# Roots of two norms moved to queries and scores, one half's query moved ahead, first picks listed in two parts

## What is computed

```
h = rmsnorm(x, norm_xa_g)            # x * rsqrt(mean(x*x) + eps) * g
x = x + softmax((h @ w_q) k^T * 128**-0.5) v @ w_o      # 4 heads of 128
h = rmsnorm(x, norm_ffn_g)
q = h @ peer_w_q                     # 8 heads, two halves of 128
s1, s2 = top16 of q . subkeys        # 128 keys for each half
top16 of the 256 sums s1 + s2  ->  experts e, g = softmax(top scores)
a = gelu(h . w_down[e]);  x = x + sum(g * a * w_up[e])
out = rmsnorm(x, final_g)
```

## Time and profile before

| | us |
|---|---|
| median of 3 runs (lowest to highest) | 1367.7 (1366.07 to 1367.84) |
| the profiled execution | 1363.8 |
| its span, first to last instruction | 1362.0 |
| TensorE busy | 1211.0 |
| VectorE busy | 931.7 |
| ScalarE busy | 521.3 |
| GpSimd busy | 292.9 |

### The profile page before, as it was taken

How to read it: one execution, slowest core, us unless ns; L and a number is a source line. 1 busy time by engine, 2 the same in 40 slices (tenths; PEclk the granted TensorE clock), 3 DMA queues, 4 the chain that set the end, 5 groups by cost and what they waited for, 6 DMA issues and landing times.

```text
span 1362.0 us, 17457 instructions
## 1 busy us (share of the span) xinstructions
PE 1211.0 (89%) x6452; PEld 885.4 (65%) x6452; DVE 931.7 (68%) x1815; ACT 521.3 (38%) x959; POOL 292.9 (22%) x261
## 2 busy tenths in 40 slices
PE   6999999999999999999898999898777777878775
PEld 7999998899988899998674555444232222323322
DVE  6765748876664675567687777767777776776655
ACT  4843236545543446645643322323222222222212
POOL 0000000000000000000024445455444444444420
PEclk9999999999999999999999999999999999999999
DMA  7554235544565645348649999999999999999994
GB/s 274 183 172 141 94 110 214 194 152 180 178 228 198 211 165 180 133 179 293 248 192 419 414 420 419 419 420 420 418 421 420 420 419 419 421 420 419 420 421 185
DMA packets 55787, 396.75 MB, mean 291 GB/s; under 512 B 6304, under 2 KB 6304, under 8 KB 8352
## 3 DMA queue, kind: packets, MB, share of 16 engines
q0 software_dynamic: 36864, 268.45, 47.6%
q1 hardware_dynamic: 17136, 119.42, 24.7%
q10 hardware_dynamic: 1712, 7.87, 1.6%
HBM read 394.67 MB, written 1.05 MB: 291 GB/s over the span
## 4 chain that ended last, share of the span: by engine, by line
PE 57%; DMA 28%; DVE 9%; ACT 4%; issue 2%; POOL 0%; DVEq 0%; SPq 0%; POOLq 0%; ACTq 0%
DMA R<-experts,IDX 28%; PE ps L534 25%; PE ps L1063 12%; PE ps L617 10%; PE ps L584 3%; DVE w_lo L1597 2%; PE ps L546 2%; DVE JUNK L2266 1%; PE ps L726 1%; PE ps L714 1%; ACT DIAG L1476 1%; ACT w_hi L1113 1%; PE ps L652 0%; DMA raw<-weights 0%; DVE eq L2243 0%
## 5 line engine op out<-in xcount | busy, mean ns | idle before, releaser
L1063 PE MATMUL ps<-R,DIAG 128*128 128x512 f32 x1020 | 479.4, 616 | 118.6 <-ACT DIAG L1476 118.4
L1063 PEld LDWEIGHTS ps<-R,DIAG 128*128 128x128 f32 x1020 | 189.0, 194 | 387.3 <-issue 195.8
L2420 POOL DMA_INDIRECT R<-experts,IDX x256 | 291.5, 1139 | 548.6 <-PE ps L1063 303.8
L2266 DVE CUSTOM_DVE_ANT_0 JUNK<-R,XN 128x1024 f32<-128x1024 f32 x256 | 313.6, 1225 | 138.7 <-DMA R<-experts,IDX 135.9
L1597 DVE TENSOR_TENSOR w_lo<-raw,w_hi 128x1024 fp32r<-128x1024 f32 x206 | 243.2, 1224 | 98.9 <-ACT w_hi L1113 95.6
L1113 ACT ACTIVATE w_hi<-raw 128x1024 fp32r<-128x1024 f32 x206 | 206.2, 1050 | 89.7 <-DMA raw<-weights 87.2
L534 PE MATMUL ps<-opC_lo,w_hi 128*128 128x256 f32 x544 | 155.3, 286 | 3.7 <-DVE opC_lo L1567 2.4
L534 PE MATMUL ps<-opC_hi,w_hi 128*128 128x256 f32 x544 | 154.7, 284 | 0.0
L534 PE MATMUL ps<-opC_hi,w_lo 128*128 128x256 f32 x544 | 154.6, 284 | 0.0
L1476 ACT ACTIVATE DIAG<-con,coef 128x128 f32<-128x128 f32 x255 | 88.6, 394 | 122.6 <-DVE coef L2276 122.3
L1468 ACT ACTIVATE act_d<-dots 128x2 f32<-128x2 f32 (+1 forms) x130 | 26.3, 203 | 273.6 <-DVE dots L2266 273.5
(11 more groups left out here) (352 smaller groups left out, 1643.4 us busy)
## 6 DMA issues: line engine op xcount, KB each, us to landing
raw<-weights SPq DMA_DIRECT2D x104, 1024.0 KB, 4.8
PQW<-weights SPq DMA_DIRECT2D x6, 1024.0 KB, 8.0
R<-experts,IDX POOLq DMA_INDIRECT x256, 31.4
LNR<-rows ACTq DMA_DIRECT2D x3, 1024.0 KB, 5.1
XF<-xT SPq DMA_DIRECT2D x2, 512.0 KB, 6.2
raw<-weights SPq DMA_DIRECT2D x2, 512.0 KB, 6.9
MEM<-mem ACTq DMA_DIRECT2D x1, 1024.0 KB, 7.7
XR<-x ACTq DMA_DIRECT2D x1, 1024.0 KB, 4.8
```

The costliest lines, as they stand in the source:

```text
L1063: mm = pe.matmul(psum[:, 4 + 2 * m + n, :], DIAG[:, k, :], rows_[:, D + n * 512:D + (n + 1) * 512], start=(it % 8 == 0 and k == 0), stop=True,
L2266: dve.tensor_tensor_reduce(out=JUNK[:, :], in0=rows_[:, 0:D], in1=XN[:, it // 8, :], scale=1.0, scalar=0.0, op0=ALU.mult, op1=ALU.add, acc ...
L2420: pool.indirect_dma_start(out=R[u][:, :], out_offset=None, in_=experts, in_offset=bass.IndirectOffsetOnAxis(ap=IDX[:, it, k:k + 1], axis=0 ...
```

## The change

The rows XN hold XR x gain only. The factor 1/root goes into the copies that follow: cross queries (QN), pick scores (SC) and the gelu's argument; rst holds it until then. scale_side becomes inverse_side, XN is not read and written again. turn_side transposes one column half at a time, as soon as its gain is there. side_half is one half block of side, so that TensorE's order can weave half 0's cross query between half blocks of the projection. Unit 11 goes to pick 0, unit 18 to pick 1, unit 8 to pick 2 once the cross values of half 1 are done. Step 0 is decoded in two parts of eight picks into eq0, with index writing IDX, and GpSimd waits for each part. In the tail the two gain multiplies write XN and the first stands ahead of the root.

```diff
         XO_END = half_end(PQ0 - 1)
-        OPENED = {0: (8, None), 1: (11, None), 2: (18, None)}
+        VALUES_END = "values"
+        OPENED = {0: (11, None), 1: (18, None), 2: (8, VALUES_END)}
         for n, u in enumerate((1, 2, 5, 6, 12)):
...
         R = {u: unit(f"R{u}", u, [P, 2 * D]) for u in sorted(_uses)}
+        eq0 = unit("eq0", 17, [P, 2, 16, 16], off=4096)
         DIAG = unit("DIAG", 19, [P, TOPK, P])
...
                 if name == "h4Ta":
-                    wait_wide(pe, "xo", 2)
+                    wait_wide(pe, "xo", 1 + j)
                 elif a >= 2 and not (name in TURNED and j >= 2):
...
             both_sides("wo2", opC, "m2")
-            side("wo2", opC, 1, 0)
-            side("wo2", opC, 1, 1, lambda: turn_side("h3T", 0, 0, 1))
-            cross_query(0, [(0, 0), (0, 1), (1, 0), (1, 1)])
-            turn_side("h3T", 2, 1, 2)
+            side_half("wo2", opC, 1, 0, 0, 0)
+            side_half("wo2", opC, 1, 0, 0, 1)
+            turn_side("h3Ta", 0, 0, 0, 1)
+            side_half("wo2", opC, 1, 0, 1, 0)
+            side_half("wo2", opC, 1, 0, 1, 1)
+            cross_query(0, [(0, 0), (0, 1)])
+            turn_side("h3Ta", 1, 0, 1, 2)
+            side_half("wo2", opC, 1, 1, 0, 0)
+            cross_query(0, [(1, 0), (1, 1)])
+            side_half("wo2", opC, 1, 1, 0, 1)
             query_turn(0)
+            side_half("wo2", opC, 1, 1, 1, 0)
             cross_scores(0, 0)
             cross_scores(0, 1)
-            cross_query(1, [(0, 0), (0, 1)])
+            side_half("wo2", opC, 1, 1, 1, 1)
+            turn_side("h3Tb", 0, 1, 0, 3)
             cross_turn(0, 0)
             cross_turn(0, 1)
-            cross_query(1, [(1, 0)])
+            cross_query(1, [(0, 0)])
             cross_values(0)
-            cross_query(1, [(1, 1)])
+            turn_side("h3Tc", 0, 1, 1, 4)
+            cross_query(1, [(0, 1), (1, 0), (1, 1)])
             has_lo(pe, "ax", 0)
...
             side("xo", AXo, 1, 0)
+            turn_side("h4Ta", 0, 0, 0, 5)
             cross_scores(1, 0)
             cross_scores(1, 1)
-            turn_side("h4Ta", 0, 0, 3)
+            turn_side("h4Ta", 1, 0, 1, 6)
             query(0, 0)
...
             head_scores(2, 0)
-            turn_side("h4Tb", 0, 1, 4)
+            turn_side("h4Tb", 0, 1, 0, 7)
+            turn_side("h4Tb", 1, 1, 1, 8)
             query(3, 0)
...
                 act.activation(rst[:, m:m + 1], rst[:, m:m + 1], ACT.Sqrt).then_inc(xn_sd, 1)
-                act.wait_ge(xn_r, turn)
-                act.activation(XN[:, m, 512:D], XN[:, m, 512:D], ACT.Copy, scale=rst[:, m:m + 1]
-                               ).then_inc(xn_act, 1)
             def cross_rows(m):
...
                     act.wait_ge(half_done, 2)
-                drain(act.activation(QN[:, m, :], bank(RING["xq"] + m), ACT.Copy), "xq", m)
+                act.wait_ge(xn_r, 1 + m)
+                drain(act.activation(QN[:, m, :], bank(RING["xq"] + m), ACT.Copy, scale=rst[:, m:m + 1]),
+                      "xq", m)
             def cross_across(m):
...
             square_side("wo2", 1, 0, 0)
+            ahead(xq)
+            hi_side(0, 0)
             square_side("wo2", 2, 1, 0)
-            ahead(xq)
+            upper_half(xq + 1, 0)
             square_side("wo2", 3, 0, 1)
+            upper_half(xq + 1, 1)
+            hi_side(0, 1)
             root_side(1, 0)
-            upper_half(xq + 1, 0)
-            hi_side(0, 0)
-            hi_side(0, 1)
-            upper_half(xq + 1, 1)
-            upper_half(xo, 0)
-            square_side("wo2", 4, 1, 1)
-            root_side(2, 1)
-            act.dma_start(LNR[:, 0, :], rows[7:8, :].rearrange("a n -> (a n)").partition_broadcast(P)
-                          ).then_inc(rows2_in, 16)
             cross_rows(0)
-            hi_side(1, 0)
-            hi_side(1, 1)
             cross_across(0)
...
             cross_exps(0, 1)
+            hi_side(1, 0)
+            cross_turned(0, 0)
+            upper_half(xo, 0)
+            act.wait_ge(xn_gain, 4)
+            act.dma_start(LNR[:, 0, :], rows[7:8, :].rearrange("a n -> (a n)").partition_broadcast(P)
+                          ).then_inc(rows2_in, 16)
+            square_side("wo2", 4, 1, 1)
+            warm(ACT.Sqrt)
+            hi_side(1, 1)
+            root_side(2, 1)
+            values_hi(0)
             upper_half(xo, 1)
-            cross_turned(0, 0)
             upper_half(xo + 1, 0)
             upper_half(xo + 1, 1)
-            values_hi(0)
             cross_rows(1)
             cross_across(1)
-            warm(ACT.Sqrt)
             square_side("xo", 1, 0, 0)
+            rows_across("h4Ta", 0)
             square_side("xo", 2, 0, 1)
             root_side(3, 0)
-            rows_across("h4Ta", 0)
             warm(ACT.Exp)
...
                 name = scores_of(j, m)
+                act.wait_ge(xn_r, 3 + m)
                 drain_aux(act.activation(SC[:, m, 2 * j:2 * j + 2, :], v3(batch(act, *name)[:, 0:T], 2),
-                                         ACT.Copy), *name)
+                                         ACT.Copy, scale=rst[:, m:m + 1]), *name)
             def gate_exp(it):
...
                 act.wait_ge(dot_done, it * TOPK + k1)
-                act.activation(act_d[:, par, k0:k1], dots[:, par, k0:k1], ACT.Gelu_apprx_tanh
-                               ).then_inc(gelu_done, 1)
+                act.activation(act_d[:, par, k0:k1], dots[:, par, k0:k1], ACT.Gelu_apprx_tanh,
+                               scale=rst[:, it // 8:it // 8 + 1]).then_inc(gelu_done, 1)
                 if it == 15 and k0 == TOPK - 1:
...
                 cs = slice(512 * g, 512 * g + 512)
-                st.do(dve.tensor_tensor(XN[:, m, cs], XR[:, m, cs], LNR[:, row, cs], ALU.mult))
+                dve.tensor_tensor(XN[:, m, cs], XR[:, m, cs], LNR[:, row, cs], ALU.mult).then_inc(xn_gain, 1)
             def mean_side(turn, m):
...
                                   ).then_inc(xn_ms, 1)
-            def scale_side(turn, m):
+            def inverse_side(turn, m):
                 dve.wait_ge(xn_sd, turn)
-                st.sync()
                 dve.reciprocal(rst[:, m:m + 1], rst[:, m:m + 1]).then_inc(xn_r, 1)
-                dve.wait_ge(xn_r, turn)
-                dve.tensor_scalar(XN[:, m, 0:512], XN[:, m, 0:512], rst[:, m:m + 1], None, ALU.mult
-                                  ).then_inc(xn_dve, 1)
             def cross_max(m, n):
...
                 drain_aux(dve.tensor_copy(H4[:, 4:8, m * P:(m + 1) * P], v3(batch(dve, name, 1), 4)), name, 1)
-            ahead_low(BLOCK["wo2"] + 3)
+            xq, xo = BLOCK["xq"], BLOCK["xo"]
+            low(BLOCK["wo2"] + 3, 0)
             dve.wait_ge(rows2_in, 16)
-            for m in range(MT):
-                residual_side("wo2", 1 + m, m, 0)
-            for m in range(MT):
-                gain_side(0, m, 0)
-            ahead_low(BLOCK["xq"])
+            residual_side("wo2", 1, 0, 0)
+            gain_side(0, 0, 0)
+            low(BLOCK["wo2"] + 3, 1)
+            low(xq, 0)
+            lo_side(0, 0)
+            low(xq, 1)
+            residual_side("wo2", 2, 1, 0)
             residual_side("wo2", 3, 0, 1)
+            gain_side(0, 0, 1)
+            low(xq + 1, 0)
+            lo_side(0, 1)
+            low(xq + 1, 1)
             mean_side(1, 0)
-            gain_side(0, 0, 1)
-            scale_side(1, 0)
-            lo_side(0, 0)
-            lo_side(0, 1)
-            ahead_low(BLOCK["xq"] + 1)
-            residual_side("wo2", 4, 1, 1)
-            mean_side(2, 1)
-            gain_side(0, 1, 1)
-            scale_side(2, 1)
-            low(BLOCK["xo"], 0)
-            lo_side(1, 0)
-            lo_side(1, 1)
+            gain_side(0, 1, 0)
+            inverse_side(1, 0)
             cross_max(0, 0)
...
             cross_weights(0, 1)
+            lo_side(1, 0)
             cross_turned(0, 1)
-            low(BLOCK["xo"], 1)
+            residual_side("wo2", 4, 1, 1)
+            gain_side(0, 1, 1)
+            low(xo, 0)
+            lo_side(1, 1)
+            mean_side(2, 1)
             values_lo(0)
-            low(BLOCK["xo"] + 1, 0)
-            low(BLOCK["xo"] + 1, 1)
+            inverse_side(2, 1)
+            low(xo, 1)
+            low(xo + 1, 0)
+            low(xo + 1, 1)
             residual_side("xo", 1, 0, 0)
...
             residual_side("xo", 2, 0, 1)
+            gain_side(1, 0, 1)
+            rows_across("h4Ta", 0)
             mean_side(3, 0)
-            gain_side(1, 0, 1)
-            scale_side(3, 0)
-            rows_across("h4Ta", 0)
+            inverse_side(3, 0)
             cross_max(1, 0)
...
                 st.then(dve.max(cv[:, 0:8], cflat))
-                st.then(dve.match_replace(sW[:, :], cv[:, 0:8], cflat, LOWEST))
-            def top_d(it):
+                if more:
+                    st.then(dve.match_replace(sW[:, :], cv[:, 0:8], cflat, LOWEST))
+            def top_d(it, more=True):
```

(59 more changed lines are left out.)

79 lines of the change are left out of this document (40 added, 39 removed).

## The result

The changed kernel takes 1360.63 us (median of 5 runs, 1359.59 to 1361.05); the kernel before, in its runs beside it, 1367.7 (1364.7 to 1369.0). The ratio is 0.9949, 95% interval 0.9933 to 0.9966: 7.0 us less, where 3.6 were forecast. The profiled execution of the changed kernel took 1360.63 us, its span 1358.9. Against the *profiled* execution of before (1363.8 us) that is 3.2 us.

What follows compares the result with a forecast made beforehand. The gather stream of 256 picks was taken to bound the kernel, early picks held by sums: 3.0 us from the earlier start and sums plus 0.6 from the tail gave 3.6, so 1367.7 became 1364.1 us, range 1360.0 to 1369.2.

Steps and rivals of the forecast that it cites:

- TensorE's wait for the third query's copy: Ahead of the sums TensorE waits 1.7 us, until 702.2 us, for the copy of half 0's third query.
- pairs of 128 elements: Decode of eight picks: two operations on 128 elements take about 0.5 us, so one decode takes 2.35 us.
- The walk: New engine order followed step by step from the old trace, good to 1.2 us: 3.6 us gained, 1364.1 us; chance 0.50.
- The release: Sums free the slots of picks 8 to about 30, so of the first list's 6.4 us lead 3.0 reach the end.
- 6.1 us as the least landing: A gather with nothing queued ahead takes at least 6.1 us from issue to landing; pick 9 lands at 723.2 us.
- the 3.4 us of the rival: Landing behind an empty queue takes 3.4 us at least; pick 9 lands at 720.5 us, kernel 1361.1 us; chance 0.15.
- The order edit: Half 0 first in TensorE's order: scores 4.5 us earlier, but the output projection of half 0 only 0.5 us earlier.
- The fall of the clock: Behind TensorE's 1.61 us gap before the first query, clock 0.50 loses 1.7 us, which the roots edit removes.
- Against which time: 3.6 us off the profiled 1363.8 gives 1360.2; the runs' median, 3.9 higher at 1367.7, gives the predicted 1364.1 us.
- The clock didn't fall ahead of the sums: Rival: clock falls behind TensorE's 1.7 us wait, sums start 1.8 us earlier instead of 3.2, 1365.5 us; chance 0.20.
- in the gaps of the new order: Rival: clock falls in TensorE's five gaps of 646 to 668 us, 1.7 us each, up to 1370.9 us; chance 0.07.
- the decode wasn't at its upper bound: Rival: each decode of eight picks takes 1 us longer (bound 3.4 us), gain 1.6 us, 1366.1 us; chance 0.08.

Runs made afterwards that it cites:

- earlyonly: The kernel before with the early list of 8 picks and its units alone: 1364.70 us against 1362.82, ratio 1.0007 (0.9998 to 1.0016).
- onelist: The changed kernel with the first 16 picks decoded in one piece again: 1358.96 us, ratio to the kernel before 0.9977 (0.9968 to 0.9987).
- before_again: The kernel before, unchanged, on a second occasion: 1362.65 us (1361.86 to 1365.35, 11 runs).
- after_again: The changed kernel, unchanged, on a second occasion: 1360.62 us (1359.64 to 1362.02, 11 runs), ratio to the kernel before 0.9987.
- roots: The kernel before with the roots edit alone (no order, early list or tail edit): 1359.59 us against 1362.82, ratio 0.9973 (0.9963 to 0.9983).
- rootstail: The kernel before with the roots edit and the tail edit alone, old order and one list: 1359.53 us (1358.01 to 1360.83, 5 runs).
- rootstail_again: The same kernel as rootstail, unchanged, on a fourth occasion: 1357.6 us (1357.16 to 1359.66, 5 runs), ratio to the kernel before 0.9966.
- onelist9: The changed kernel with one decode of 16 picks and the units of picks 1 and 2 exchanged: 1359.24 us, ratio to the kernel before 0.9971.
- before_third: The kernel before, unchanged, a third time, on another chip: 1367.17 us (1365.51 to 1369.5, 11 runs).
- fill: The kernel before with 14 unread transposes in TensorE's gap ahead of half 0's last transposes: 1362.98 us against 1362.82, ratio 1.0001 (0.9992 to 1.0010).

## Why the prediction was right, and where its sum was off

| step | forecast | measured |
|---|---|---|
| output projection of half 0 | 668.6 | 668.67 |
| query done, ScalarE's copy | 680.8, 681.8 | 680.94, 681.82 |
| first maxima | 683.4 | 683.58 |
| first gather | 690.5 | 690.64 |
| gather of pick 3 | 697.2 | 697.07 |
| TensorE's wait for the third query's copy | 1.7 | 1.62, clock 1.00 |
| coefficients, first sums | 706.35, 707.3 | 706.36, 707.39 |
| gather of pick 9 | 717.1 | 717.01 |
| pairs of 128 elements | 0.5 | 0.49 |

*The walk* held to 0.2 us at every point on the clock, the pairs of the decode among them. Part of this is luck: I walked from the trace of before, and the execution of after happened to reach the common start 0.37 us sooner (635.43, 635.80). Counted from there, the first gather and the first sums are 0.5 us later than forecast (forecast +54.7 and +71.5, measured +55.21 and +71.96). The Trainium skill (VectorE: DVE Perf Modes, the section on the TRN2 errata) asks for tiles of 512 elements or more, because of a fixed latency in each operation. The trace agrees: two operations of 128 elements take 0.49 us, one of 512 takes 0.69, and with the early list there are two decodes of such operations where there was one of 3.0 us. The rule spoke against this edit, and the runs agree with it: the list in two parts brought nothing.

*The release.* That an early list isn't worth more than the queue was right, and stronger than I put it: alone it gained nothing (earlyonly), and without it the changed kernel was no slower (onelist). Its size was too high: of the first list's lead I let 3.0 us reach the last row, and from before to after 2.3 us did (+715.55, +713.27), with the fall of the clock in before counted in. Against before_again, which had no fall there, it is 0.5 us, or 1.1 with after_again (+712.65). 6.1 us as the least landing was nearly right: 5.9, 5.7 and 5.5 us were seen behind an empty queue, never the 3.4 us of the rival. The 4.4 us that the Trainium skill gives (DMA: Bandwidth & Descriptors, Anatomy of one DMA) was not met either.

*The order edit*, forecast at 0.5 us, has the right time on the clock (668.67) by luck: counted from the common start the output projection comes at +33.24, in before at +33.26. On top of the roots edit it has the wrong sign at this place: all three traces of kernels with the old order and the roots edit start the stage earlier, roots by 1.8 us, rootstail and rootstail_again, which had the clock's fall on the way, by 0.2. What I compared was before against all edits together; the roots edit alone had already shortened the gaps in front of the output projection (0.83, 0.49, 1.14 and 0.78 us in before; 1.28, 0.78 and 0.17 in roots). What the order costs in the whole time is not shown: onelist, with order and tail, is 1.4 us slower than rootstail_again, roots with tail alone (1358.96, 1357.6), but on another chip and with overlapping intervals, and onelist9 beside roots on one chip is the same to 0.4 us (1359.24, 1359.59), though it has the tail edit and roots has not.

*The fall of the clock.* I counted 1.7 us for the fall behind the gap of 1.61 us. It did cost about that in before (1.8 us at the last row), but I took it as a property of the kernel, and the same gap did no harm in before_again. My sum against the profiled execution still came out (3.6, measured 3.2 on the clock, 2.7 from the common start), since that execution had the fall and was spared the one at the end. On the one occasion at the lower level where both kernels ran, the gain of the medians is 2.2 us.

*Against which time.* Here the step failed that cost most. I took the 3.9 us between the profiled execution of before (1363.8) and its median (1367.7) as something that the changed kernel has too. It hasn't: its profiled execution and its median are both 1360.63 us, within 0.5 us of 1363.8 - 3.6 = 1360.2. In before_third such 4 to 5 us are one stop of ScalarE. That the runs of the first comparison had the same stop is a conclusion from their level, not seen: the only trace of that occasion of the kernel before is of an execution without it. The range reached to 1360.0 and held the time, by luck: I had set that end for gathers that land faster, which they did not, and the time came there because 3.9 us were added that the changed kernel doesn't have.

*The other rivals.* The clock didn't fall ahead of the sums, nor in the gaps of the new order; the decode wasn't at its upper bound.

*Open:* what stops ScalarE. The DMA view of before_third has one block of code loaded at 701.6 us, near the start of its stop; that of rootstail has none within 8 us before its stop at 698.6 to 701.5 us, nor during it. And before_again has such a block at 700.9 us and no stop. So in these traces the stop neither needs the loading of code nor always comes with it. Both stops fall in the first 12 us of the gather stream, at the same instruction. Why the changed kernel didn't stop in any of its three traces or by any median, though it passes the same place, is not known.

## What to carry to other kernels

Compare the profiled execution with the median before you subtract anything: a difference of 3.9 us, more than the whole gain that I forecast, was something that the trace didn't hold. Don't take one trace's clock for the kernel's either: two traces of one kernel ended within 0.3 us of each other, each with another fall of the clock in it. In a stream that lives on slots, work out which sum frees which slot before you make the list earlier; a decode that delays those sums costs more than it brings. Of a change in several parts, run each alone: here one part (roots off the rows) gives 3.2 us, more than the whole change on a like occasion (2.2), the tail 0.6 in the traces, and without the other two the kernel had its lowest median (1357.6 us).

## What the runs showed of the hardware

A gap of TensorE of the same length had both outcomes: 1.61 us ahead of the query with the clock at 0.50 behind it (before) and at 1.00 (before_again); 2.25 us ahead of the last sums with 0.50 behind it in three traces (before_again, fill, after_again) and 1.00 in five; gaps of 1.28 and 0.78 us one after the other with a fall twice (rootstail, rootstail_again) and without (roots). A copy or a gelu on ScalarE with a scale for each partition takes 0.09 us more than one without: 0.47 instead of 0.38 us for SC, 0.29 instead of 0.20 us for act_d. And an engine can stand still for 2.9 to 4.4 us with nothing ahead of it that the profile names (rootstail, before_third). On that chip this was so in every run of the kernel before, if their times are a guide (1364.8 us or more); on three other chips the same kernel has a median of 1362.6 to 1362.9 us.
